# Sparse attention in a fused transformer layer: keys and values formed per head instead of queries and outputs in the latent space, and one more top-k inside the attention loop

## The chip, the cores and the metric

The kernel runs on one core of a Trainium2 chip. The metric is the device time of one execution in microseconds (us), lower is better. Before the change three executions took 1062.2, 1065.04 and 1066.31 us; the median is 1065.04 us.

## The reference, cut to what matters

One decoder layer on 512 tokens of width 1024: modulated RMSNorm, sparse attention beside a pooling mixer, both gated, an output projection, and then a mixture of 32 experts. The change touches only the attention (`SEQ` 512, `N_HEADS` 8, `HEAD_DIM` 64, `KV_LATENT` 128, `Q_BLOCK` 128, so `k_sel` is 128):

```python
score = einsum('bqhs,bqh->bqs', relu(raw), wi_b * IDX_W_SCALE)
score = where(causal[None], score, -inf)
_, idx = lax.top_k(score, k_sel)
kv_sel = vmap(lambda kv, i: kv[i])(ckv, idx)
q_lat = einsum('bqhd,lhd->bqhl', q_b, w_uk)
logits = einsum('bqhl,bqkl->bqhk', q_lat, kv_sel) * ATTN_SCALE
p = softmax(where(valid, logits, -inf))
o_lat = einsum('bqhk,bqkl->bqhl', p, kv_sel)
return einsum('bqhl,lhd->bqhd', o_lat, w_uv)
```

For a head, `q_lat . kv` is the same number as `q . (w_uk kv)`, and `(p kv) w_uv` the same as `p (kv w_uv)`. The order of the products can be chosen.

## The kernel before, in words

All of it is one program with an in-order instruction stream for each engine, written out by hand. There is no planner. Results of TensorE (PE) go through eight banks of PSUM. The list `JOBS` (lines 257 to 299) gives every PE result a number in the order in which PE makes them, and names the engine that empties it: "A" for ScalarE (ACT), "D" for VectorE (DVE). Job n lies in bank n % 8, and `start` (line 1549) makes PE wait until job n - 8 has been emptied. So the order of this list decides which old result a new one waits for.

Tokens come in four chunks of 128. A query of chunk ch sees keys 0 to 128 (ch + 1) - 1. The stages that matter, in the order of PE:

- `tok` (line 1611): the latent (`ckv`), the indexer's queries and keys and its weights, for each chunk; `uk` turns w_uk round; `tr` turns ckv and the indexer's operands (line 1621).
- `index_chunk(ch)` (line 1625): indexer products of chunk ch in four row groups. ACT takes their relu (line 867) into two alternating buffers, and DVE sums them with weights in `select(ch)` (lines 1163 and 1166). `take_best` (line 1178) is then one round per 8 of the 128 best: a MAX8 and a MATCH_REPLACE8 over the scores. Then one TENSOR_SCALAR makes the additive mask `bias_of[ch]`. Chunk 0 needs no choice. Chunk 1 is chosen in `select(1)`, chunk 2 in `select(2)`, both before the attention loop. Chunk 3 is only scored there (`apart=True`), and its 16 rounds are spread over iterations 0 to 4 of the loop (`TAKES`, line 1199).
- `q`, `pool`, `gb` and `ga` are projections "in parts" (`by_feature_parts`, line 1633): each weight block of 128 columns is split into a high and a low part. ACT writes the high part (`block_high`, line 841). The low part is a subtraction that GpSimd (POOL) does for `q`, `pool` and `gb` (`block_low`, line 648), and DVE for `ga` (line 1233). A block is 24 matmuls of 128x512.
- `qlat` (line 1653): per head, the query through w_uk: 8 fp32 matmuls that use 64 rows of PE each, two side by side.
- `ada` (line 1592), 12 pieces of the modulation vector, their row sums `row` (`ada_sum`, line 1667), added on DVE in `ada_rows` (line 1195).
- The attention loop (PE line 1685, ACT line 909, DVE line 1237) has 8 iterations g: chunk g // 2, four of the eight heads. In iteration g PE does: `PT` (line 1691, turn the four heads' probabilities, each waits for DVE), `L` of g + 1 (`logits`, line 1677, four fp32 matmuls over all 128 rows, 128 (ch + 1) keys wide), `O` (line 1697, one fp32 matmul of 128x512 per key block, the four heads side by side), `gb` of g + 1, in g 0 the four `z`, in odd g a `V` (line 1711, output through w_uv), in g 1 `ada_sum` 4 to 7, and in g 0 to 3 one `ada`. DVE does in iteration g: scale the four heads' exponentials (`RECIPROCAL` and `TENSOR_SCALAR`, lines 1242 and 1243), in g 2 `ada_rows`, then `maxima(g + 1)` (line 1209: mask, row maximum; this empties the logits), then its rounds of `TAKES`. ACT does: copy the `PT` results, copy `O`, exponentials of g + 1 (line 899), tanh of `gb` and the next `block_high` (lines 903 and 841).
- After the loop: 8 blocks `B` (96 matmuls), `ada_sum` 8 to 11, then the blocks `ga` and `A`, the output projection, the router and the experts. In the last iteration (g 7) ACT and DVE also split `zT` and the first weights of `B` (lines 919, 874, 1219, 1226); `B` waits for that.

POOL builds the pooled inputs dT (lines 664 to 670) between its `block_low` steps. It loads the bias rows (line 677) once the four `z` are done, and then does `block_low` of gb 2 and gb 3 back to back.

Of the kernel before, what the change touches and what calls it, by code (L numbers as in the profile page):

```python
# [27 lines left out]
P = 128  # L28
# [5 lines left out]
LAT = 128  # L34
# [32 lines left out]
def trunk(nc, x, c, norm1_g, norm2_g, w_ada, b_ada, w_in, kv_norm_g, w_uk, w_uv, w_pool, pool_scale,  # L67
# [3 lines left out]
    with ctx:  # L71
# [17 lines left out]
        T3 = sb("T3", [P, 3, T])  # L89
        ckv = sb("ckv", [P, C, LAT])  # L90
        wi = sb("wi", [P, C, IH])
        uvp = sb("uvp", [P, H, P])
# [63 lines left out]
        q_latT = hT  # L156
# [3 lines left out]
        dT = qT  # L160
# [7 lines left out]
        o_latT = attn[:, 2048:3072].rearrange("p (h q) -> p h q", h=H)  # L168
# [13 lines left out]
        uk = small[:, 0:512]  # L182
        ukT = area_b[:, 512:1024].rearrange("p (i t) -> p i t", i=4)
# [66 lines left out]
        def piece(kind, i=0):  # L250
# [9 lines left out]
                + [("tok", i, "D") for i in range(C)] + [("uk", 0, "A")] + [("tr", i, "A") for i in range(C)]  # L260
                + [("idx", 4 + i, "A") for i in range(4)]
                + [("q", 0, "A"), ("q", 1, "A"), ("ada", 4, "A"), ("q", 2, "A"), ("q", 3, "A"), ("ada", 5, "A")]
                + [("qlat", h, "A") for h in range(H)]
# [4 lines left out]
        JOBS += [("L", i, "D") for i in range(4)] + [("gb", 0, "A")]  # L268
        for g in range(NGR):
# [8 lines left out]
            if g % 2:  # L278
                JOBS += [("V", g // 2, "A")]
            if g == 1:  # L280
                JOBS += [("row", j, "D") for j in range(4, 8)]
            if g < 4:
                JOBS += [("ada", 8 + g, "A")]
        JOBS += [("B", m, "D") for m in range(KD)]
        JOBS += [("row", j, "D") for j in range(8, 12)]
# [17 lines left out]
        def bank(kind, i=0):  # L303
            return ps[:, number[kind, i] % 8, :]
# [277 lines left out]
        def _(pool):  # L582
# [16 lines left out]
            link(nc.gpsimd.memset(uvp[:, :, :], 0.0))  # L599
# [35 lines left out]
            for h in range(H):  # L635
                at = HD * (h % 2)
                pool.dma_start(uvp[:, h, at:at + HD], w_uv[0, :, h, :]).then_inc(uv_in, 16)
# [17 lines left out]
            for g, w in enumerate(WINDOWS):  # L655
                block_low(block_no["pool", g] + 2)
                pool.wait_ge(by_act, emptied[number["pool", g]])
                if g == 0:
                    pool.wait_ge(job_done, number["qlat", H - 1] + 1)
# [22 lines left out]
            pool.wait_ge(job_done, number["V", C - 1] + 1)  # L682
# [110 lines left out]
        def _(act):  # L793
# [58 lines left out]
            nc.scalar.activation(ukT[:, :, :].rearrange("p a l -> p (a l)"), job("uk"), ACT.Copy).then_inc(by_act, 1)  # L852
# [24 lines left out]
            index_chunk(1)  # L877
            for i in range(4):
# [4 lines left out]
            for h in range(H):  # L883
                nc.scalar.activation(q_latT[:, h, :], job("qlat", h), ACT.Copy).then_inc(by_act, 1)
# [21 lines left out]

            exponentials(0)
            gate_b(0)
            for g in range(NGR):
# [13 lines left out]
                if g == 0:  # L923
                    act.wait_ge(d_ok, PG)
                nc.scalar.activation(o_latT[:, 4 * hh:4 * hh + 4, :].rearrange("p h q -> p (h q)"),
                                     job("O", g), ACT.Copy).then_inc(by_act, 1)
# [7 lines left out]
                if hh:  # L934
                    nc.scalar.activation(oT[:, :, ch * P:(ch + 1) * P],
                                         job("V", ch).rearrange("p (a q) -> p a q", a=4),
                                         ACT.Copy).then_inc(by_act, 1)
# [158 lines left out]
        def _(dve):  # L1096
# [56 lines left out]
            def select(ch, apart=False):  # L1153
# [3 lines left out]
                s = score[:, 0:n]  # L1157
                for h in range(IH):
# [5 lines left out]
                    else:  # L1164
                        to = r if apart and h == IH - 1 else s
# [21 lines left out]
            select(2)  # L1187
# [10 lines left out]
            last_scores = relu[:, 1, :]  # L1198
            TAKES = (3, 4, 3, 3, 3)
# [37 lines left out]
            for g in range(NGR):  # L1237
# [7 lines left out]
                if g == 2:  # L1245
                    dve.wait_ge(brow_in, 32)
                    for j in range(4, 8):
                        ada_rows(j)
                if g < NGR - 1:
                    maxima(g + 1)  # L1250
# [4 lines left out]
                if g < len(TAKES):  # L1255
                    take_best(last_scores, TAKES[g])
                if g == len(TAKES) - 1:
                    link(v.tensor_scalar(bias_of[C - 1], last_scores, 2 * MASKED, HIDDEN, ALU.is_gt, ALU.mult))
# [10 lines left out]
            for j in range(8, 12):  # L1269
# [709 lines left out]
```

## Time and profile before

| | us |
|---|---|
| median of three executions | 1065.04 |
| profiled execution, its own time | 1059.28 |
| its span in the profile | 1057.4 |
| TensorE busy (share) | 988.0 (93%) |
| VectorE busy (share) | 781.2 (74%) |
| ScalarE busy (share) | 558.6 (53%) |
| GpSimd busy (share) | 212.3 (20%) |

Times in the views count from the start of the span. The indexer and `q` begin near 61 us, the attention loop near 130 us. The loop's last `gb` block ends at 229.49 us, `B` runs to 260.48 us, and the part with the experts takes the rest from about 400 us on. A matmul's shown duration contains its latency, so the shown durations of neighbours overlap; the distance of starts, or the merged pieces of the chain of waits, gives the rate. One fp32 matmul counts as two instructions there.

### The profile page before, as it was taken

To read this page: it belongs to the slowest core of one execution; us is meant where nothing else is said; L and a number is where in the kernel's file an instruction comes from. 1 tells how busy PE (TensorE), PEld (TensorE's weight loads), DVE (VectorE), ACT (ScalarE), POOL (GpSimd) and SP (SyncE) were. 2 spreads that over 40 slices of the span, in tenths; PEclk is the share of its full clock that TensorE was granted. 3 is DMA by queue.
4 is the path that set the end of the run, shared out by engine and by line. 5 is a ranking of instruction groups with operands and counts; after the bars stand their busy time and mean duration, and the time that the engine had idled before them with its cause. 6 is when DMAs were issued, how large, how long until landed. Compare 5 with 4: busy or idle time off the path is not lost.

```text
span 1057.4 us, 13833 instructions
## 1 busy us (share of the span) xinstructions
PE 988.0 (93%) x4467; PEld 665.7 (63%) x4467; DVE 781.2 (74%) x1116; ACT 558.6 (53%) x840; POOL 212.3 (20%) x237
## 2 busy tenths in 40 slices
PE   3889899999999983899999999999999999999995
PEld 2666566667887553566666666666666665666652
DVE  0474967535435657789898898889989889898885
ACT  6334443543223232466675666756666675766742
POOL 1233931105100012111211212121121211212100
PEclk9899999999999995899999999999999999999998
DMA  9826625502306457479999999999999999999745
GB/s 345 294 81 239 239 81 205 188 6 95 133 27 239 162 220 247 160 281 365 380 341 382 363 369 363 353 376 359 364 358 357 374 356 362 363 361 366 240 129 195
DMA packets 63208, 283.29 MB, mean 268 GB/s; under 512 B 7488, under 2 KB 8796, under 8 KB 38600
## 3 DMA queue, kind: packets, MB, share of 16 engines
q1 hardware_dynamic: 53528, 257.93, 65.2%
q0 software_dynamic: 9648, 24.94, 9.0%
q8 instruction: 19, 0.31, 0.1%
q14 instruction: 13, 0.11, 0.0%
HBM read 272.62 MB, written 18.56 MB: 275 GB/s over the span
## 4 chain that ended last, share of the span: by engine, by line
PE 85%; DVE 5%; DMA 4%; issue 2%; ACT 2%; POOL 0%; SPq 0%; DVEq 0%; ACTq 0%; POOLq 0%
PE ps L1828 32%; PE ps L1563 19%; PE ps L1890 10%; PE ps L1884 8%; DMA X<-in_w_down_dram 3%; PE ps L1762 2%; PE ps L1773 2%; PE ps L1592 2%; PE ps L1799 2%; PE ps L1611 2%; PE ps L1677 2%; PE ps L1806 1%; PE ps L1864 1%; DVE whl L1302 1%; DMA X<-in_x_dram 1%
## 5 line engine op out<-in xcount | busy, mean ns | idle before, releaser
L1828 PE MATMUL ps<-whl,xhl 128*96 128x512 f32 x1536 | 369.6, 399 | 0.0
L1302 DVE TENSOR_TENSOR whl<-ring,whl 128x1024 fp32r<-128x1024 f32 x256 | 304.2, 1221 | 53.5 <-ACT whl L961 52.6
L1828 PEld LDWEIGHTS ps<-whl,xhl 128*96 128x96 f32 x1536 | 250.3, 163 | 108.3 <-issue 0.4
L961 ACT ACTIVATE whl<-ring 128x1024 fp32r<-128x1024 f32 x256 | 267.4, 1060 | 56.2 <-PE ps L1828 47.4
L1563 PE MATMUL ps<-h_hi,wb_hl 128*128 128x512 f32 x384 | 127.1, 404 | 1.2 <-POOL wb_hl L648 1.2
L1890 PE MATMUL ps<-X,attn 128*96 128x512 f32 x256 | 115.4, 594 | 0.7 <-DMA X<-in_w_down_dram 0.7
L729 POOL DMA_INDIRECT moe_rows<-mix,ius x31 | 46.3, 1494 | 298.6 <-DVE mix L1445 150.2
L1884 PE MATMUL ps<-whl,ahl 128*96 128x512 f32 x384 | 97.2, 402 | 2.9 <-DVE whl L1302 2.9
L1563 PEld LDWEIGHTS ps<-h_hi,wb_hl 128*128 128x128 f32 x384 | 72.9, 190 | 22.2 <-issue 5.1
L1302 DVE TENSOR_TENSOR whl<-X,whl 128x1024 fp32r<-128x1024 f32 x64 | 78.3, 1225 | 8.8 <-ACT whl L961 7.9
L961 ACT ACTIVATE whl<-X 128x1024 fp32r<-128x1024 f32 x64 | 67.9, 1062 | 20.0 <-PE ps L1828 20.0
L1890 PEld LDWEIGHTS ps<-X,attn 128*96 128x96 f32 x256 | 41.6, 164 | 57.3 <-issue 51.1
L1884 PEld LDWEIGHTS ps<-whl,ahl 128*96 128x96 f32 x384 | 60.4, 164 | 26.0 <-issue 3.1
L1563 PE MATMUL ps<-h_lo,wb_hl 128*128 128x512 f32 x192 | 75.7, 394 | 0.0
L1035 ACT ACTIVATE attn<-ps 128x192 f32<-128x192 f32 x32 | 10.6, 330 | 91.4 <-PE ps L1864 91.4
L648 POOL TENSOR_TENSOR wb_hl<-ring,wb_hl 128x1024 fp32r<-128x1024 f32 x16 | 38.5, 2414 | 90.1 <-ACT wb_hl L841 72.1
L1445 DVE SCALAR_TENSOR_TENSOR mix<-ps,WC,attn 96x512 f32<-96x512 f32 x64 | 44.8, 740 | 10.7 <-PE ps L1890 10.7
L759 POOL COPY ius<-idx 128x1 uint32 (+1 forms) x31 | 14.3, 460 | 161.4 <-DMA moe_rows<-mix,ius 161.4
L1563 PE MATMUL ps<-zo_hl,wb_hl 128*128 128x512 f32 x192 | 44.9, 390 | 0.0
L723 POOL DMA_INDIRECT apad<-h_rows,iug x32 | 39.7, 1241 | 25.0 <-POOL iug L750 24.4
L841 ACT ACTIVATE wb_hl<-ring 128x1024 fp32r<-128x1024 f32 x24 | 25.2, 1055 | 36.6 <-PE ps L1563 32.7
L1563 PEld LDWEIGHTS ps<-h_lo,wb_hl 128*128 128x128 f32 x192 | 36.5, 190 | 9.0 <-issue 1.9
(248 smaller groups left out, 1169.7 us busy)
## 6 DMA issues: line engine op xcount, KB each, us to landing
ring<-in_w_gu_dram SPq DMA_DIRECT2D x128, 1024.0 KB, 9.8
X<-in_w_down_dram SPq DMA_DIRECT2D x64, 1024.0 KB, 10.2
ring<-in_w_ada_dram SPq DMA_DIRECT2D x12, 2048.0 KB, 12.0
ring<-in_w_in_dram SPq DMA_DIRECT2D x6, 2048.0 KB, 8.0
ring<-in_w_out_dram SPq DMA_DIRECT2D x2, 2048.0 KB, 8.1
X<-in_x_dram SPq DMA_DIRECT2D x1, 2048.0 KB, 8.0
ring<-in_w_b_up_dram SPq DMA_DIRECT2D x1, 2048.0 KB, 14.2
ring<-in_w_a_up_dram SPq DMA_DIRECT2D x1, 2048.0 KB, 8.0
```

Of the source, the lines that this page charges most:

```text
L648: nc.gpsimd.tensor_tensor(wb_hl[:, buffer_of(BLOCKS[n]), 1, :, :], block_w(n), wb_hl[:, buffer_of(BLOCKS[n]), 0, :, :], ALU.subtract).then ...
L723: pool.indirect_dma_start(out=XG[0:slots, b, :], out_offset=None, in_=h2_dram, in_offset=bass.IndirectOffsetOnAxis(ap=iug[0:slots, b:b + 1 ...
L729: pool.indirect_dma_start(out=y_dram, in_=Y[0:slots, b, :], in_offset=None, out_offset=bass.IndirectOffsetOnAxis(ap=which, axis=0), bounds ...
L841: nc.scalar.activation(wb_hl[:, buffer_of(BLOCKS[n]), 0, :, :], block_w(n), ACT.Copy).then_inc(b_hi_ok, 1)
L961: nc.scalar.activation(whl[:, buf, 0, :], part, ACT.Copy).then_inc(hi_ok, 1)
L1302: v.tensor_tensor(whl[:, buf, 1, :], part, whl[:, buf, 0, :], ALU.subtract).then_inc(lo_ok, 1)
L1445: last = v.scalar_tensor_tensor(out=Y[0:slots, b, sl], in0=ps[0:slots, 2 + half, :], scalar=WC[0:slots, b:b + 1], in1=g2b[0:slots, sl], op ...
L1563: last = mm(out_, a, b, start=(n == 0 and start_), stop=(n == len(pairs) - 1))
L1592: last = mm(b_[at:at + 32, :], cnd[:, 2, k:k + 1].broadcast_to([P, 32]), w[:, k, :], start=(k < 4), stop=(k >= 4), tile_position=(0, at))
L1828: last = mm(ps[0:slots, half, :], xhl[:, a, k, :], whl[:, at, b, half * CH:(half + 1) * CH], start=False, stop=(k == KD - 1 and a == 1))
L1884: last = mm(ps[0:slots, 2 + half, :], ahl[:, a, i, :], whl[:, at, b, half * CH:(half + 1) * CH], start=(i == 0 and a + b == 0), stop=False)
L1890: last = mm(ps[0:slots, 2 + half, :], actT[:, k, :], down_part(k)[:, half * CH:(half + 1) * CH], start=False, stop=(k == KF - 1))
```

## The change

Keys per head (`kT`: four matmuls, w_uk by ckvT) are formed once after `index_chunk(1)`, and values per head (`V`: four matmuls, ckvT by w_uv) once after the first logits. `uk`, `qlat` and the four `V` of the loop go. `L` takes 64 rows of PE per head, even and odd heads in the two row halves. `O` is done per head with 64 columns of weights and 128 of queries, even and odd heads in the two column halves, and gives the attention output itself. Chunk 2 is now only scored before the loop; its 16 rounds are done in iterations 0 and 1, and those of chunk 3 in iterations 2 to 4. `ada_sum` 8 to 11 move from behind `B` into iteration 5, their additions on DVE into iteration 6. The banks of all jobs are shifted by the same number so that the last job keeps its bank.

```diff
-        T3 = sb("T3", [P, 3, T])
-        ckv = sb("ckv", [P, C, LAT])
+        V = sb("V", [P, C, AW])
-        uvp = sb("uvp", [P, H, P])
+        uvp = sb("uvp", [P, 2, AW])
...
-        q_latT = hT
+        T3 = V[:, 0:3, :]
+        ckv = V[:, 3, :].rearrange("p (c l) -> p c l", c=C)
+        kT = hT[:, 0:PG, :]
-        dT = qT
+        dT = hT[:, PG:2 * PG, :]
...
-                + [("tok", i, "D") for i in range(C)] + [("uk", 0, "A")] + [("tr", i, "A") for i in range(C)]
-                + [("idx", 4 + i, "A") for i in range(4)]
+                + [("tok", i, "D") for i in range(C)] + [("tr", i, "A") for i in range(C)]
+                + [("idx", 4 + i, "A") for i in range(4)] + [("kT", a, "A") for a in range(PG)]
-                + [("qlat", h, "A") for h in range(H)]
-        JOBS += [("L", i, "D") for i in range(4)] + [("gb", 0, "A")]
+        JOBS += [("L", i, "D") for i in range(4)] + [("V", s_, "A") for s_ in range(C)] + [("gb", 0, "A")]
-            if g % 2:
-                JOBS += [("V", g // 2, "A")]
+            if g == 5:
+                JOBS += [("row", j, "D") for j in range(8, 12)]
-        JOBS += [("row", j, "D") for j in range(8, 12)]
-            return ps[:, number[kind, i] % 8, :]
+            return ps[:, (number[kind, i] - len(JOBS)) % 8, :]
...
             index_chunk(1)
+            act.wait_ge(h_lo_ok, 1)
+            for a in range(PG):
+                nc.scalar.activation(kT[:, a, :], job("kT", a), ACT.Copy).then_inc(by_act, 1)
-            for h in range(H):
-                nc.scalar.activation(q_latT[:, h, :], job("qlat", h), ACT.Copy).then_inc(by_act, 1)
+            act.wait_ge(job_done, number["V", C - 1] + 1)
+            for s_ in range(C):
+                nc.scalar.activation(V[:, s_, :], job("V", s_), ACT.Copy).then_inc(by_act, 1)
             exponentials(0)
             gate_b(0)
-                nc.scalar.activation(o_latT[:, 4 * hh:4 * hh + 4, :].rearrange("p h q -> p (h q)"),
-                                     job("O", g), ACT.Copy).then_inc(by_act, 1)
+                nc.scalar.activation(oT[:, 2 * hh:2 * hh + 2, ch * P:(ch + 1) * P],
+                                     job("O", g)[:, 0:2 * P].rearrange("p (a q) -> p a q", a=2),
+                                     ACT.Copy).then_inc(by_act, 1)
...
-            select(2)
+            select(2, apart=True)
             select(3, apart=True)
-            TAKES = (3, 4, 3, 3, 3)
+            scores_of = {2: bias_of[2], 3: relu[:, 1, :]}
+            TAKES = ((2, 8, False), (2, 8, True), (3, 5, False), (3, 6, False), (3, 5, True))
+                if g == 6:
+                    for j in range(8, 12):
+                        ada_rows(j)
                 if g < len(TAKES):
-                    take_best(last_scores, TAKES[g])
-                if g == len(TAKES) - 1:
-                    link(v.tensor_scalar(bias_of[C - 1], last_scores, 2 * MASKED, HIDDEN, ALU.is_gt, ALU.mult))
+                    sc, times, whole = TAKES[g]
+                    take_best(scores_of[sc], times)
+                    if whole:
+                        link(v.tensor_scalar(bias_of[sc], scores_of[sc], 2 * MASKED, HIDDEN, ALU.is_gt, ALU.mult))
...
+            pe.wait_ge(uk_in, 16)
+            for a in range(PG):
+                mm(start("kT", a), uk[:, a * P:(a + 1) * P], ckvT, start=True, stop=True).then_inc(job_done, 1)
-                    mm(b_[:, 0:P * (ch + 1)], q_latT[:, h, ch * P:(ch + 1) * P], ckvT[:, 0:P * (ch + 1)], start=True,
-                       stop=True).then_inc(job_done, 1)
+                    r = slice(HD * (h % 2), HD * (h % 2) + HD)
+                    mm(b_[:, 0:P * (ch + 1)], qT[r, h // 2, ch * P:(ch + 1) * P], kT[r, h // 2, 0:P * (ch + 1)], start=True,
+                       stop=True, tile_position=(HD * (h % 2), 0)).then_inc(job_done, 1)
             logits(0)
+            pe.wait_ge(uv_in, 16)
+            for s_ in range(C):
+                mm(start("V", s_), ckvT[:, s_ * P:(s_ + 1) * P], uv, start=True, stop=True).then_inc(job_done, 1)
             gate_b(0)
-                chain(b_, [(ckv[:, s, :], pT[:, s, :, :].rearrange("p h q -> p (h q)")) for s in range(ch + 1)], job_done)
+                for a in range(2):
+                    for s in range(ch + 1):
+                        for q in range(2):
+                            h, at = 4 * hh + 2 * a + q, HD * q
+                            last = mm(b_[at:at + HD, a * P:(a + 1) * P], V[:, s, h * HD:(h + 1) * HD], pT[:, s, 2 * a + q, :],
+                                      start=(s == 0), stop=(s == ch), tile_position=(0, at))
+                if g == 5:
+                    for j in range(8, 12):
+                        ada_sum(j)
-            for j in range(8, 12):
-                ada_sum(j)
```

## Rows read from the trace of the kernel before

**Rows 1.** The page, the chain that ended last, shares of the span.

```profile
PE 85%; DVE 5%; DMA 4%; issue 2%; ACT 2%; POOL 0%; SPq 0%; DVEq 0%; ACTq 0%; POOLq 0%
```

**Rows 2.** Chain of waits in order of time: start us, length us, what.

```profile
62.58 12.77 PE ps L1563 x48
...
90.20 3.63 PE ps L1653 x16
...
128.21 0.29 DVE attn L1209
...
144.80 1.85 PE ps L1592 x16
146.66 0.59 PE ps L1691 x4
...
200.81 1.31 PE ps L1691 x12
...
217.16 3.44 PE ps L1677 x8
...
229.49 0.02 issue
...
236.66 23.82 PE ps L1563 x112
260.48 3.44 PE ps L1667 x8
```

**Rows 3.** Groups by shape up to 330 us: busy us, mean ns, idle before.

```profile
L1563 PE MATMUL ps<-attn,ckv 128*128 128x512 f32 x40 | 18.8, 600 | 1.0 <-ACT attn L914 1.0
L1563 PE MATMUL ps<-attn,uvp 128*128 128x128 f32 x64 | 7.9, 276 | 0.8 <-ACT attn L925 0.8
```

**Rows 4.** Timeline of PE: start us, length us, in brackets idle before.

```profile
62.58 0.47 PE L1563 MATMUL ps<-h_hi,wb_hl 128*128 128x512 f32 x1 [1.20 <-POOL wb_hl L648]
```

**Rows 5.** Windows of the trace: length, busy time by engine, PE's granted clock.

```profile
64.00:65.00 1.00, 1.00 (x3) 0.73 (x3) 1.00 (x1) 0.00 (x0) 0.82 (x1) 0.50 0.19 74
...
134.00:134.50 0.50, 0.50 (x4) 0.50 (x4) 0.43 (x5) 0.00 (x0) 0.00 (x0) 0.50 0.00 0
```

**Rows 6.** Timeline of DVE: top-k rounds of widths 384 and 512.

```profile
98.56 0.56 DVE L1180 MAX8 top<-small 128x8 f32<-128x384 f32 x1
...
99.81 0.56 DVE L1180 MAX8 top<-small 128x8 f32<-128x384 f32 x1
...
178.90 0.69 DVE L1180 MAX8 top<-small 128x8 f32<-128x512 f32 x1
...
180.40 0.69 DVE L1180 MAX8 top<-small 128x8 f32<-128x512 f32 x1
```

**Rows 7.** Timeline of DVE: the other steps of an iteration.

```profile
159.94 2.58 DVE L1195 TENSOR_TENSOR small<-ps,small 1x512 f32<-1x512 f32 x4
...
176.06 0.56 DVE L1209 CUSTOM_DVE_ANT_0 attn<-ps,maskb 128x384 f32<-128x384 f32 x1 [3.28 <-PE ps L1677]
...
176.78 0.56 DVE L1209 CUSTOM_DVE_ANT_0 attn<-ps,maskb 128x384 f32<-128x384 f32 x1
...
183.44 0.16 DVE L1242 RECIPROCAL am<-am 128x1 f32<-128x1 f32 x1
...
183.97 0.15 DVE L1242 RECIPROCAL am<-am 128x1 f32<-128x1 f32 x1
```

**Rows 8.** Timeline of all engines: DVE and POOL at 156 us, ACT before.

```profile
155.86 1.05 ACT L841 ACTIVATE wb_hl<-ring 128x1024 fp32r<-128x1024 f32 x1
...
156.85 0.35 DVE L1243 TENSOR_SCALAR attn<-attn,am 128x256 f32<-128x256 f32 x1
...
156.99 2.42 POOL L648 TENSOR_TENSOR wb_hl<-ring,wb_hl 128x1024 fp32r<-128x1024 f32 x1 [5.67 <-ACT wb_hl L841]
...
157.31 2.25 DVE L1243 TENSOR_SCALAR attn<-attn,am 128x256 f32<-128x256 f32 x1
```

**Rows 9.** Timeline of POOL behind the four z.

```profile
146.61 4.71 POOL L648 TENSOR_TENSOR wb_hl<-ring,wb_hl 128x1024 fp32r<-128x1024 f32 x2
```

## What the change will do: the prediction

> **What bounds the kernel now.** I read the page's chain first: PE holds 85% of the span [rows 1]. Then the chain in order of time, from the indexer to the end of `B` [rows 2]. PE follows PE almost throughout. The one stretch where another engine decides is 118 to 133 us, when DVE scores chunk 3 and starts the first maxima at 128.21. From 146.66 (start of the turns of iteration 1) to 229.49 (end of the last `gb`) PE is never released by DVE. So work taken from PE shortens the kernel until DVE becomes late, and the question is how much room DVE has when 16 more rounds come into the loop. The groups by shape [rows 3], the windows with the clock [rows 5] and the timelines of DVE and POOL [rows 6 to 9] give the prices.
>
> **PE, what goes and what comes.** `qlat` goes, 3.63 us [rows 2]. `uk` is four turns at 0.11 (1.31 / 12), 0.44 [rows 2]. `L`: 3.44 for four heads of 512 keys [rows 2], by width 0.86 (ch + 1), and two of each, 17 us. `O`: 20 matmuls of 0.86 (an `ada_sum` of four such takes 3.44 [rows 2]), 17 us. `V`: 32 small ones, 64 instructions at 0.107 (this is the rate of the first 16 of the 112 in [rows 2]), 6.8 us [rows 3]. `kT` and `V` are new, 3.44 each. If row halves and column halves run side by side, `L` and `O` cost half, 8.6 each. `qlat` shows it for row halves: eight matmuls of 512 in 3.63, half of 8 x 0.86. `ada` shows it for column groups: eight of 512 columns in 1.85, a quarter of 6.9 [rows 2]. PE sheds 45 and gains 24: 21 us less work. The trace has no fp32 matmul of 64 weight columns with 128 moving ones. Its price lies between half of 0.214 (perfectly paired) and the whole 0.214 that the unpaired 128x128 costs. I take half and keep the other end below as a rival.
>
> Each `L` and `O` now changes the shape in which PE is divided. `ada` with its two such changes takes 1.85 where a quarter of 8 x 0.853 is 1.71, so about 0.07 a change [rows 2]. The Trainium skill (TensorEngine Tiling (Array Packing), section Key Properties) says that changing the tiling mode drains TensorE, which speaks against this change. By the row, the nine changes where PE is the bound below would add 0.6 us. By a drain as long as a whole 128-column matmul (0.21) it would be 2 us. No row separates the drain from the matmul, and the sum leaves it out.
>
> **Before the loop.** PE idles 1.20 us before `q` [rows 4]; `kT` fills it. So the first maxima move by -3.63 - 0.44 - 1.20 + 3.41 = -1.9. The clock adds to this. At 64 us PE is granted 0.50, the 1.2 GHz level [rows 5], after idling between the turns. Two blocks with an `ada` there (a block is 24 matmuls at 0.227, from 96 of them in some 22 us behind 238 [rows 2]) take 12.77 for the blocks where 10.9 is full speed, so it costs 1.7. With `kT` in the gap it may stay at 2.4 GHz (-3.5 in all) or not (-1.9); I take -2.7. The eight ACT copies of `qlat` become four of `kT` and hide under `q`. Scoring chunk 2 alone frees DVE at about 98, which gains nothing, since chunk 3 waits for PE. DMA: one issue for w_uv in place of eight on POOL at 40 us, hidden.
>
> **The first iteration, the bank.** `gb` 0 ran while DVE scored. It is now number 8 behind `L` 0, so its bank is that of `L` 0, and it waits for the first maxima to empty it. `V` fills 3.4 of the shadow, then PE idles some 2.9 us and `gb` 0 (5.45) is exposed. It ends at 128.21 - 2.7 + 0.3 + 5.45 = 131.3. Such an idle stretch preceded the 0.50 at 134 us [rows 5]; a slow stretch costs up to 1.7, I take 1.2: G = 132.5. Queued behind it on PE are the four turns and `L` of iteration 1, for which DVE waits; on ACT, tanh, `block_high` and the copies of the turns.
>
> **The loop, DVE.** A round is 1.25 at width 384 and 1.51 at 512 [rows 6]. Scaling four heads is 4 x 0.53 = 2.1 at 384, maxima 4 x 0.72 = 2.85 [rows 7]. A narrower chunk saves about 0.13 a head and step, by the two MAX8 widths [rows 6]. `ada_rows` is 2.6 [rows 7]. Between the last scaled head and the next maxima lie a turn and the first `L`, 0.8 to 1.2. Let S(g) be the start of scaling in iteration g.
> - S(1) = G + 1.05 + 1.8 + 8 x 1.25 = G + 12.85. PE needs 13.8 to `ada` 8's end, about level.
> - S(2) = S(1) + 1.6 + 0.8 + 2.3 + 10.0 + 0.4 (mask) = + 15.1.
> - S(3) = + 1.9 + 2.6 + 2.3 + 5 x 1.51 = + 14.4.
> - S(4) = + 1.9 + 1.1 + 2.85 + 6 x 1.51 = + 14.95.
> - S(5) = + 2.1 + 1.2 + 2.85 + 7.6 + 0.45 = + 14.2.
>
> PE needs only 12.5, 9.9, 10.3 and 9.3 in these four (turns, halved `L` and `O`, `gb` 5.45, `ada_sum` 3.44, `ada` 1.85). So PE waits 16 us and DVE is the bound: 58.65 where PE took 54.15 before (146.66 to 200.81 [rows 2]). S(5) = 132.5 + 12.85 + 58.65 = 204.0.
>
> **Two prices on top.** First, a TENSOR_SCALAR of DVE that meets POOL's `block_low` waits for its end: 2.25 in place of 0.35, over at 159.56, POOL at 159.41 [rows 8]. The MAX8 at 512 keep their 0.69, so only masks and scaling are exposed. POOL starts 1.75 after a `gb` block ends (tanh and the 1.05 of ACT [rows 8]). With PE done early and DVE's scaling last, the two meet: worked out, scaling 3 meets `gb` 5's step (about 1.7), mask and scaling 5 meet `gb` 7's (1.6), scaling 4 just misses (0.4). In iteration 1 POOL's double step begins 1.8 after the last `z` (144.80, 146.61 [rows 2, 9]), at G + 13.7, in the middle of scaling 1 (G + 13.0 to 14.4). That costs 0 to 4.7, I take 2.9. Together 6.6, with bounds 0 and 11. Second, the clock: PE idles 1.5 to 4 us in each of iterations 2 to 5, and turns and `L` on DVE's path then run at 1.2 GHz, 0.3 to 0.9 each: 1.6, bounds 0 and 4. S(5) = 212.2.
>
> **The rest.** From S(5) PE is the bound again: scaling and turns 2.6, `L` 1.7, `O` 1.3, `gb` 5.45, `ada_sum` 3.44, turns 1.75, `L` 1.7, `O` 1.7, `gb` 5.45 = 25.1, and 1.5 for one slow stretch (bounds 0 and 1.7). The last `gb` ends at 238.8, before 229.49 [rows 2]: +9.3. Behind it `B` waited until 238.4 (236.66 and the 16 small matmuls). Without `V` its start is set by ACT splitting zT, DVE's part of it and the first weights, some 1 us sooner. But PE idles 3.4 us there, and a slow stretch takes 1.3 back: +0.3. `ada_sum` behind `B` is gone, -3.44 [rows 2]; the first `ga` weights must be ready without its cover, and by the rates (ACT 1.05, DVE 1.2 after block 6 of `B`) they just are; missing it costs under 1. From there all is as before. Sum: +9.3 + 0.3 - 3.4 = **+6.2**. The profiled execution took 1059.28 (span 1057.4), so it would become 1065.5. The median of the runs is 1065.04, 5.8 above it, and I put the same difference on it: **1071**.
>
> **Rivals.**
> - *Ports and clock miss.* DVE bounds the loop as above, but `block_low` falls between the scalings and PE stays at 2.4 GHz. Without the extras: first maxima -3.5, G = 130.5, last `gb` 227.1 (-2.4), tail -1.05, `ada_sum` -3.44: -6.9 at best, 1058; with some of them, up to 1065; 1061 stands for it. For it: before, only one scaling in the loop was hit for long. Against: PE had no idle time there then.
> - *PE's saving comes through.* If DVE hid its rounds, PE's 16 us of waiting would be saved on top of -6.9, about 1043. Against: DVE's sums are of durations that hardly vary.
> - *The low clock feeds itself (slower).* In iterations 1 to 4 PE has 2.6 to 5 us to spare. A slow stretch costs 1.7, as the first one did, two cost 3.4; where an iteration has as much as 7 us at 1.2 GHz the slack is used up and `gb` ends late, POOL's step with it. Price: 1.5 an iteration more, +6 on the forecast, 1077. For it: both low windows of [rows 5] followed idle stretches as short as those here. Against: PE is mostly busy after each.
> - *The halves don't overlap* as written. DVE's path hardly feels it (one head of `L` is no slower), but iterations 5 and 6 pay 3.4 for `L` and 3.0 for `O`: 1077.5. Against: `qlat` and `ada`.
>
> **Numbers.** Forecast 0.47 (own range 1066 to 1076), ports and clock miss 0.25, saving through 0.05, low clock 0.17, halves 0.06. A measurement tells about 0.5% (5.3 us) from no change. Of the forecast 0.27 lies above 1070.3, with the last two that makes slower 0.50. Of the first rival 0.10 lies below 1059.7, with the second faster 0.15. The same: 0.35. The range leaves out the second rival and the outer tails: 1058 to 1080.
>
> **What would show it.** In the changed profile: DVE nearly unbroken from the first maxima 1 to scaling 5; PE idle before the turns of iterations 2 to 5, released by DVE line 1243; `gb` 0 released by the maxima; granted clock of 0.5 in several windows between 125 and 245; TENSOR_SCALARs of 1 to 2.4 us beside `block_low`; last `gb` at 235 to 242. It is wrong if PE's busy tenths stay at 9 through the loop, or if the last `gb` ends before 230.

## The result and the profile after

The changed kernel takes 1072.32 us (median of four runs, 1072.27 to 1072.45) where the kernel before, run beside it, takes 1065.22: a ratio of 1.0099, 95% interval 1.0073 to 1.0124. A later job gave 1071.58 against 1061.0, ratio 1.0095 [1.0069, 1.012]. It is slower by about 1%. The forecast was 1071, in a range of 1058 to 1080.

The profiled execution took 1072.3, its span is 1070.0. That is 12.6 more than the span of before, while the medians lie 7.1 and 10.6 apart: the profiled execution of before (1059.28) was one of its quicker ones.

The shares of the chain that ended last, to be held against [rows 1], and the page's busy times and granted clock of the changed kernel:

```profile
PE 981.7 (92%) x4519; PEld 657.7 (61%) x4519; DVE 787.2 (74%) x1116; ACT 556.0 (52%) x835; POOL 205.3 (19%) x229
PEclk9899989989999997789999999999999999999998
PE 81%; DVE 10%; DMA 3%; issue 3%; ACT 2%; POOL 0%; SPq 0%; DVEq 0%; ACTq 0%; POOLq 0%
```

PE lost 4 points of the chain, and DVE has 10% of it. Next comes that chain in order of time (start, length, what), to be held against [rows 2]:

```profile
128.13 5.75 PE ps L1558 x24
147.23 5.33 DVE attn L1236
152.69 1.24 PE ps L1683 x3
153.93 1.20 PE ps L1666 x4
182.45 1.57 DVE attn L1236
186.19 2.45 PE ps L1666 x8
215.32 1.72 DVE maskb L1255
217.82 2.79 PE ps L1683 x12
220.62 2.68 PE ps L1666 x8
223.30 1.46 PE ps L1694 x24
224.76 5.68 PE ps L1558 x24
230.44 3.44 PE ps L1654 x8
239.44 5.70 PE ps L1558 x24
253.05 6.98 PE ps L1558 x23
```

L1558 is a block or its part, L1683 the turns, L1666 `L`, L1694 `O`, L1654 `ada_sum`, L1236 DVE's scaling, L1255 the mask; the last line is the first blocks of `B`. The first line is `gb` 0, released by the first maxima as forecast. Between 147 and 217 us the chain runs through DVE (scaling, maxima, rounds), and PE has only the turns and `L` between the scaling and the next maxima in it. The last `gb` ends at 239.44 + 5.70 = 245.1; before it ended at 229.49.

What PE waited for between 118 and 250 us (us in total, number of waits, longest):

```profile
PE ps L1683 <- DVE attn L1236: 16.1, 5, 5.1
PE ps L1558 <- DVE am L1202: 2.5, 1, 2.5
PE ps L1694 <- ACT attn L910: 1.2, 1, 1.2
```

The forecast had PE waiting 16 us for DVE in iterations 2 to 5. It waited 16.1, but in all five iterations from 1 to 5, and 4.6 of it in iteration 1. That the two numbers agree is in part luck.

The windows of before, then of after (from:to, length; busy us of PE, PEld, DVE, ACT, POOL with counts; granted clock; DMA share; GB/s):

```profile
118.00:250.00 132.00, 127.00 (x599) 86.59 (x598) 82.52 (x234) 61.54 (x148) 38.94 (x30) 0.99 0.35 124
```

```profile
118.00:250.00 132.00, 110.21 (x618) 71.10 (x617) 100.19 (x272) 58.04 (x142) 29.77 (x22) 0.92 0.34 120
216.00:218.00 2.00, 0.17 (x1) 0.21 (x2) 1.89 (x5) 0.00 (x0) 0.74 (x1) 0.50 0.12 13
218.00:220.00 2.00, 2.00 (x11) 1.98 (x11) 1.19 (x5) 0.98 (x2) 0.00 (x0) 0.50 0.89 285
220.00:222.00 2.00, 2.00 (x7) 1.06 (x8) 0.00 (x0) 0.98 (x2) 0.00 (x0) 0.50 1.05 410
```

In this stretch DVE is busy 17.7 us more, PE 16.8 us less, and the granted clock falls from 0.99 to 0.92. The 16.8 us are mostly waits, not saved work: of the whole execution PE is busy 981.7 us, before 988.0. The three small windows show how this is paid. PE is idle (0.17 of 2 us) behind DVE's mask and scaling 5, the clock is at 0.50, the 1.2 GHz level, and there it stays while PE does the turns and `L` that DVE waits for.

The long TENSOR_SCALAR that the forecast spoke of, on DVE and with it the step of GpSimd that it met (start, length, engine, line, operation):

```profile
146.84 0.28 DVE L1236 TENSOR_SCALAR attn<-attn,am 128x128 f32<-128x128 f32 x1
147.23 5.32 DVE L1236 TENSOR_SCALAR attn<-attn,am 128x128 f32<-128x128 f32 x1
```

```profile
147.81 4.64 POOL L643 TENSOR_TENSOR wb_hl<-ring,wb_hl 128x1024 fp32r<-128x1024 f32 x2
```

Two heads of one shape: 0.28 and 5.32. The second ends at 152.55, GpSimd's two steps at 152.45. It starts at 147.23, 0.58 us before the first of the two steps in GpSimd's records; what holds it in that time the trace doesn't show.

### The profile page after: what moved, and what is told of

Its sections match the earlier page's. It is cut to its first block, busy times and chain, and to the rows that moved or that the text cites. A ratio compares the mean times of both kernels' runs of the same rounds, so it can differ in the third digit from the quotient of the medians.

```text
span 1070.0 us, 13914 instructions
## 1 busy us (share of the span) xinstructions
PE 981.7 (92%) x4519; PEld 657.7 (61%) x4519; DVE 787.2 (74%) x1116; ACT 556.0 (52%) x835; POOL 205.3 (19%) x229
## 4 chain that ended last, share of the span: by engine, by line
PE 81%; DVE 10%; DMA 3%; issue 3%; ACT 2%; POOL 0%; SPq 0%; DVEq 0%; ACTq 0%; POOLq 0%
PE ps L1820 32%; PE ps L1558 14%; PE ps L1882 10%; PE ps L1876 8%; PE ps L1754 2%; PE ps L1765 2%; PE ps L1791 2%; DVE top L1173 2%; PE ps L1606 2%; PE ps L1798 1%; PE ps L1587 1%; DMA X<-in_w_down_dram 1%; DVE small L1174 1%; PE ps L1666 1%; PE ps L1856 1%
## 5 line engine op out<-in xcount | busy, mean ns | idle before, releaser
L1558 PE MATMUL ps<-h_hi,wb_hl 128*128 128x512 f32 x384 | 123.9, 396 | 2.5 <-DVE am L1202 2.5
L1558 PEld LDWEIGHTS ps<-h_hi,wb_hl 128*128 128x128 f32 x384 | 72.2, 188 | 23.5 <-issue 5.0
L1558 PE MATMUL ps<-h_lo,wb_hl 128*128 128x512 f32 x192 | 74.9, 390 | 0.0
L1028 ACT ACTIVATE attn<-ps 128x192 f32<-128x192 f32 x32 | 10.6, 332 | 90.8 <-PE ps L1856 90.8
L1558 PE MATMUL ps<-zo_hl,wb_hl 128*128 128x512 f32 x192 | 46.4, 399 | 3.3 <-DVE wb_hl L1219 3.3
L1558 PEld LDWEIGHTS ps<-zo_hl,wb_hl 128*128 128x128 f32 x192 | 37.1, 194 | 11.3 <-issue 3.5
```

The lines of the kernel that those rows point to most:

```text
L1558: last = mm(out_, a, b, start=(n == 0 and start_), stop=(n == len(pairs) - 1))
```

## Experiments

"Ctl" is the changed kernel once more; the others are edits of it unless their text says otherwise. All ran beside the kernel before (1061.0 us in the first job, 1061.38 in the second, 1062.31 in the third, 1062.61 in the fourth). S(g) is the start of scaling in iteration g, as in the prediction. Ctl ran in the first job alone. Where a run of a later job is compared with it, its distance from its own before is given too; ctl is +10.6 us from its before.

**ctl**, unedited.

> The changed kernel itself, unedited, so that the others of this job have it beside them. Both theories: 1072 us, within 1 us of its first runs, 5 to 9 us over the kernel before.

Measured: 1071.58 (eight runs, 1068.6 to 1076.2). In its profile `gb` 0 takes 7.18 us where it took 5.75 in the first profile. The low clock falls on other pieces from run to run, so single steps are compared with that in mind.

**dve_before**: the rounds of chunk 2 go back ahead of the loop, and the heads' new form stays.

```diff
-            select(2, apart=True)
+            select(2)
...
-            TAKES = ((2, 8, False), (2, 8, True), (3, 5, False), (3, 6, False), (3, 5, True))
+            TAKES = ((3, 3, False), (3, 4, False), (3, 3, False), (3, 3, False), (3, 3, True))
```

> The changed kernel with the 16 rounds of chunk 2 back before the loop and the rounds of chunk 3 as before (3, 4, 3, 3, 3). Theory A (VectorE bounds iterations 1 to 4 of the changed kernel): VectorE's share of these iterations falls by 20 us of rounds, PE becomes the bound or nearly so (iterations of 13.8, 12.5, 11.4, 10.4 and 11.1 us), PE's idle stretches shrink, the clock stays high and the scaling no longer meets GpSimd's steps: 1052 to 1058 us, 15 to 20 under the changed kernel and under the kernel before too. Theory B (the rounds are hidden in the loop, and the loss comes from gb 0 waiting for a bank and from the new shapes of the matmuls): the rounds were free where they are, so 1069 to 1073, no gain. Before the loop both expect at most 2 us of delay, since the rounds end near 119 us and chunk 3's relu near 120.

Measured: 1052.54, ratio 0.9897 [0.9861, 0.9933]. Without the rounds in the loop the change makes the kernel 8.5 us faster than before; the rounds in the loop cost 19 us on top. The loss is DVE's in the loop. The 8.5 us are those of keys and values per head together with the moved `ada_sum` 8 to 11, which is still in this kernel; no run separates the two.

**before_top2**: the other half alone. The kernel before, with only the rounds of chunk 2 put into the loop by the lists of the changed kernel (and, as there, `select(2, apart=True)`, with the scores of chunk 2 kept in `bias_of[2]`).

```diff
-            TAKES = (3, 4, 3, 3, 3)
+            TAKES = ((2, 8, False), (2, 8, True), (3, 5, False), (3, 6, False), (3, 5, True))
```

> The kernel before with one part of the change alone: chunk 2 only scored before the loop, its 16 rounds in iterations 0 and 1, those of chunk 3 in iterations 2 to 4. PE's work stays as before. Theory A (VectorE becomes the bound wherever its chain is longer than PE's iteration): iterations 1 to 4 cost PE 15.7, 11.8, 14.5 and 12.1 us, VectorE's chain 15.1, 14.4, 14.9 and 14.2, so it adds about 5 us, and some 2 to 6 more for scaling that meets GpSimd and for the low clock: 1066 to 1072 where the kernel before takes 1061. Theory B (the rounds are hidden): within 1 us of the kernel before.

Measured: 1079.01, ratio 1.0156 [1.0117, 1.0196]. That is +17.6 against its own before, well above what was expected. The two parts together, -8.5 and +17.6, make +9.1, close to the +10.6 of ctl in the first job. The expectation (1066 to 1072) missed the size: it had 2 to 6 us in all for meetings with GpSimd and the low clock. The chain of this kernel has both (its profiled execution, 1083.09, is 4 us above its median): line 1243 is its scaling (the four longest pieces), line 1678 its `L` over all rows. The second line below is four heads of 256 keys: 3.43, where 4 x 0.43 = 1.7 is full clock ([rows 2], 0.86 for 512):

```profile
146.62 5.37 DVE attn L1243
152.57 3.43 PE ps L1678 x8
182.02 2.43 DVE attn L1243
200.37 1.21 DVE attn L1243
216.21 2.44 DVE attn L1243
```

**pool_apart**: GpSimd's low parts of `gb` 2 and `gb` 3 move ahead of its wait for `z` and the bias rows, so they are no longer back to back in front of scaling 1.

```diff
+            block_low(block_no["gb", 2])
+            block_low(block_no["gb", 3])
...
-            for n in range(block_no["gb", 2], block_no["ga", 0]):
+            for n in range(block_no["gb", 4], block_no["ga", 0]):
```

> The changed kernel with one thing moved: GpSimd does its steps for gb 2 and gb 3 before it waits for the last z and loads the bias rows, so they no longer meet VectorE's scaling in iteration 1 (a TENSOR_SCALAR of 5.3 us in the changed kernel). Theory A: 4 to 6 us faster, 1066 to 1068, and that TENSOR_SCALAR takes 0.3. Theory B (PE's own order sets iteration 1): within 1 us of the changed kernel.

Measured: 1064.87 (ten runs), 1.0035 [1.0014, 1.0056], 6.7 us less than ctl. Scaling 1 takes 0.29 a head (three of its four TENSOR_SCALARs in DVE's timeline, then GpSimd's step, which is over at 145.32, before the first head at 145.53):

```profile
145.92 0.29 DVE L1238 TENSOR_SCALAR attn<-attn,am 128x128 f32<-128x128 f32 x1
146.31 0.29 DVE L1238 TENSOR_SCALAR attn<-attn,am 128x128 f32<-128x128 f32 x1
146.71 0.28 DVE L1238 TENSOR_SCALAR attn<-attn,am 128x128 f32<-128x128 f32 x1
```

```profile
142.95 2.37 POOL L643 TENSOR_TENSOR wb_hl<-ring,wb_hl 128x1024 fp32r<-128x1024 f32 x1 [6.27 <-ACT wb_hl L836]
```

S(1) to S(2) takes 15.57 instead of the changed kernel's 21.27; the other steps stay within 0.7 us but for S(4) to S(5), 15.80 instead of 17.21. Of the 5.7 us, 5.0 are the meeting itself, and 0.7 the wait for the first `L` behind it, which the changed kernel does at the 1.2 GHz level and this one does not. DVE's wait there, in the changed kernel and in this one:

```profile
155.22 0.42 DVE L1202 CUSTOM_DVE_ANT_0 attn<-ps,maskb 128x256 f32<-128x256 f32 x1 [1.89 <-PE ps L1666]
```

```profile
148.21 0.42 DVE L1204 CUSTOM_DVE_ANT_0 attn<-ps,maskb 128x256 f32<-128x256 f32 x1 [1.22 <-PE ps L1668]
```

**gb0_first**: `gb` 0 ahead of `V` in the order of PE, so it waits for an older bank than that of `L` 0. ScalarE's exponentials and its work on `gb` 0 move ahead of its copies of `V` with it.

```diff
-        JOBS += [("L", i, "D") for i in range(4)] + [("V", s_, "A") for s_ in range(C)] + [("gb", 0, "A")]
+        JOBS += [("L", i, "D") for i in range(4)] + [("gb", 0, "A")] + [("V", s_, "A") for s_ in range(C)]
...
```

> The changed kernel with gb 0 ahead of the four V matmuls in the list of jobs, so that gb 0 runs in the shadow of the scoring and only the last V (0.9 us) waits for the first maxima. Iteration 0 then starts 3.5 us earlier. Theory A: VectorE's chain starts with it, so the whole gain arrives, or more or less than it as the scaling now meets GpSimd's steps at another place: 1067 to 1071. Theory B: about the same 3.5 us, 1068 to 1069. What tells them apart is the other kernels; this one measures the bank term, forecast at 5.5 us of exposed gb.

Measured: 1069.77 (nine runs), 1.0072 [1.0052, 1.0092], 1.8 less than ctl where 3.5 was expected; the intervals overlap. The first iteration is 1.6 us shorter (S(0) to S(1) 15.48 instead of 17.05), and scaling 1 still meets GpSimd (5.38). The exposed `gb` 0 is real but small in this kernel. In both, S(1) comes 11.76 us after the start of maxima 1 (134.88 to 146.64, here 131.88 to 143.64), the time of DVE's own maxima and rounds; what counts is only how much earlier maxima 1 can start, and behind the first maximum of all that was 1.8 us (5.32 instead of 7.11).

**warm**: PE does small matmuls without use (128x128, into a bank about to be overwritten) where it would idle ahead of the turns of iterations 1 to 5: 16, 5, 10, 14, 20 of them.

```diff
+            FILL = {1: 16, 2: 5, 3: 10, 4: 14, 5: 20}
...
+                    if i == 0:
+                        for _ in range(FILL.get(g, 0)):
+                            mm(b_[:, 0:P], ident[:, :], ones[:, :], start=True, stop=True)
```

> The changed kernel with filler matmuls of 128x128 (0.21 us each, into the bank that the turns then overwrite) on PE ahead of the turns of iterations 1 to 5: 16, 5, 10, 14 and 20 of them, where PE only waits for VectorE. It adds work and takes nothing away. If the low clock (1.2 GHz after PE idled) costs what the trace suggests, 1.2 to 2.4 us between the last scaled head and the next maxima in each of iterations 1, 3, 4 and 5 where full speed needs 0.8 to 1.2, plus slow starts of L and O: 4 to 7 us faster than the unedited changed kernel, 1065 to 1068. If the clock is only a sign and VectorE's instructions set the time by themselves: no gain, or a loss of up to 3 us where a filler runs too long.

Measured: 1072.22 (ten runs), 1.0095 [1.0067, 1.0123], +10.8 from its own before: nothing gained. By the steps, S(4) to S(5) shortened from 17.21 to 15.83 and S(5) to S(6) from 8.89 to 7.42, but S(3) to S(4) grew from 17.60 to 18.26: there the fillers stood in front of turns that were ready. The test was confounded, so it was made again.

**warm2**: fillers in iterations 1, 4 and 5 alone, in numbers that end before DVE's last scaled head.

```diff
+            FILL = {1: 16, 4: 12, 5: 18}
```

> The filler experiment again, mended: fillers only where PE idled longest (16 ahead of the turns of iteration 1, 12 in 4, 18 in 5), none in iterations 2 and 3. The first one gained 0.7, 1.3 and 1.5 us behind its fillers of iterations 1, 4 and 5, and lost 3 in iteration 3, where PE came late and the fillers stood in front of the turns. If the low clock costs what these stretches say (theory C): 2 to 4 us faster than the changed kernel's 1071.6 to 1072.3, and from the last scaled head to the next maxima in iterations 4 and 5 1.3 to 2 us in place of 2.9 and 3.3. If not: within 1 us of it.

Measured: 1067.41 (six runs), 1.0056 [1.0032, 1.008], +4.8 from its own before. That is 4.2 us less than ctl (5.8 by the distances from before), just over the expected 2 to 4. The two ran in different jobs and their intervals overlap (ctl 1.0069 to 1.012), so the size is uncertain, and the steps of the profile have to carry it. PE's timeline ahead of iteration 5, its window, and DVE's wait for the first `L`:

```profile
209.48 4.18 PE L1685 MATMUL ps<-ones,ident 128*128 128x128 f32 x36
214.65 2.19 PE L1688 MATMUL ps<-ident,attn 128*128 128x128 f32 x12 [0.99 <-DVE attn L1236]
```

```profile
216.00:218.00 2.00, 1.99 (x12) 1.07 (x12) 0.17 (x1) 1.29 (x3) 0.00 (x0) 1.00 1.00 381
```

```profile
218.04 0.69 DVE L1202 CUSTOM_DVE_ANT_0 attn<-ps,maskb 128x512 f32<-128x512 f32 x1 [1.86 <-PE ps L1666]
```

```profile
222.58 0.69 DVE L1202 CUSTOM_DVE_ANT_0 attn<-ps,maskb 128x512 f32<-128x512 f32 x1 [3.33 <-PE ps L1666]
```

The last line is the same wait in the changed kernel without fillers: DVE stands 3.33 us between its last scaled head and the first maximum at the 1.2 GHz level, 1.86 at 2.4 GHz. The waits behind scaling 1, 3, 4 and 5 are 0.7, 0.4, 0.9 and 1.5 us shorter than in the changed kernel, 3.4 together, so the low clock was part of its time. But the fillers did one thing more: scaling 3 no longer meets GpSimd's step (1.2 us) and mask 5 is 0.2 us shorter, since the two engines have shifted against each other. So about 1.4 us of what the profile gained is not the clock.

**unpaired**: dve_before with `O` ordered one column half after the other, so that no two halves can run side by side.

```diff
-                for a in range(2):
-                    for s in range(ch + 1):
-                        for q in range(2):
+                for q in range(2):
+                    for a in range(2):
+                        for s in range(ch + 1):
```

> The kernel with the rounds before the loop, in which PE is nearly the bound (1052.5 us), with the matmuls of O ordered by column half first, so that neighbours use the same half and can't run side by side. If the halves overlap as the trace suggests (16 matmuls of 128 columns in 1.90 us, 0.12 each), O takes 0.86 (ch + 1) in place of 0.43 to 0.47 (ch + 1): 8 us more PE work, 5 to 8 of it on the path, 1057 to 1060. If they don't overlap anyway: no difference, 1052 to 1053.

Measured: 1048.71, 0.9883 [0.9843, 0.9922]. This expectation fell: the kernel was not slower. The last `O` of the loop in the chains of dve_before and of unpaired:

```profile
220.40 1.90 PE ps L1694 x32
```

```profile
214.31 3.26 PE ps L1694 x32
```

16 matmuls of 128 columns take 1.90 in pairs (0.119 each) and 3.26 without (0.204 each). So the halves do overlap, and the rival that said they don't is out. But the time did not follow. From S(4) to S(6) dve_before took 25.5 us and unpaired 20.9, for two reasons. In dve_before scalings 4 and 5 each meet GpSimd's step, about 1.9 us each over the usual 0.42, and in unpaired neither does:

```profile
185.07 2.34 DVE L1236 TENSOR_SCALAR attn<-attn,am 128x384 f32<-128x384 f32 x1
198.69 2.31 DVE L1236 TENSOR_SCALAR attn<-attn,am 128x384 f32<-128x384 f32 x1
```

And the wait behind scaling 5 is 1.87 instead of 3.17, at the higher clock (that behind scaling 4 is 0.9 longer). Over 118 to 250 us the clock is 0.99 in place of 0.96. That the longer `O` kept the clock up is argued; the missed meetings, a matter of when the engines get there, weigh more. The two medians are not to be told apart (intervals overlap). The windows of dve_before and of unpaired:

```profile
118.00:250.00 132.00, 119.36 (x675) 79.80 (x674) 91.55 (x241) 60.08 (x148) 44.57 (x34) 0.96 0.35 124
```

```profile
118.00:250.00 132.00, 124.83 (x679) 88.11 (x676) 89.11 (x240) 58.46 (x146) 43.31 (x34) 0.99 0.33 116
```

**after_unpaired**: the same order in the changed kernel.

> The changed kernel with only O's matmuls ordered by column half, so that neighbours can't overlap and O costs 4 to 7 us more of PE. Where the rounds are before the loop that order was no slower, and its granted clock was 0.99 against 0.96 through the loop. Theory C (PE's idle time pulls the clock down, and work put into the idle time costs nothing and keeps it up): in the iterations that VectorE bounds the extra work is free and turns and logits run faster, in iterations 5 and 6, where PE bounds, it costs up to 3: 1067 to 1072, clock of the loop above the changed kernel's 0.92. Theory D (O's time counts wherever it stands): 4 us or more slower than the changed kernel, 1075 or more.

Measured: 1074.79, 1.0111 [1.0072, 1.0149], 3.2 us more than ctl (1.9 by the distances from before), between the two theories; the intervals overlap. The loop's clock is 0.94 instead of 0.92 (0.91 in ctl). Up to S(3), where DVE is the bound, no step changes by more than 0.03 us, so the longer `O` is hidden. S(3) to S(5) takes 1.1 us more, of it 1.2 in longer meetings with GpSimd (scaling 3 2.04 instead of 1.56, mask 5 2.42 instead of 1.71), and S(6) to S(7), where PE is the bound, 1.4 more.

**all3**, dve_before with pool_apart and gb0_first, then **all4**, with the order of unpaired too, then **all5**: in all4 the low parts of `gb` 4 to 7 move from GpSimd to DVE, behind maxima 3 to 6, so that in the loop no scaling can meet GpSimd's step for them.

```diff
-            for n in range(block_no["gb", 4], block_no["ga", 0]):
-                block_low(n)
...
+                if 2 <= g <= 5:
+                    block_low(g + 2, "gb")
```

> The changed kernel with all three edits: the rounds of chunk 2 back before the loop, GpSimd's steps for gb 2 and gb 3 ahead of the last z, gb 0 ahead of V. With the rounds gone from the loop (1052.5) the other two have less to give: the scaling of iteration 1 no longer ends last, so the GpSimd edit gives 0 to 2, the bank up to 3.5. Theory A: 1048 to 1052. Theory B, by which the bank and PE's order carry the loss, wants the full 3.5 of the bank here: 1049 or less.

> All three edits (rounds before the loop, GpSimd ahead of z, gb 0 ahead of V) and O ordered by column half. The first three gave 1050.6, the last with the rounds alone 1048.7, and there PE waited 4 us for GpSimd's gb 2 in iteration 1, which the second edit removes. Theory C: the gains add, 1045 to 1048. Theory D: 1053 or more, since O's extra time counts.

> The kernel with the four edits above, and the low parts of gb 4 to 7 taken from GpSimd and given to VectorE behind the maxima of iterations 2 to 5 (1.23 us each), so that no scaling meets a GpSimd step any more; before, scalings 4 and 5 held a TENSOR_SCALAR of 2.3 us each. If that meeting still ends last, 1 to 4 us faster than the kernel with four edits; if VectorE's extra 1.23 us an iteration ends last, 0 to 3 slower. I expect 1 to 2 faster, 1043 to 1047.

Measured: 1050.58 (0.9893 [0.9854, 0.9933]), 1049.41 (0.9894 [0.9842, 0.9945]), 1045.74 (0.9836 [0.9801, 0.9871]). The first two are not to be told from dve_before and unpaired alone: in dve_before scaling 1 meets no step of GpSimd, so the first edit has little left to give, and all4 missed its expected 1045 to 1048 slightly. All5 has the lowest median of the study, 1.6% below the kernel before and 2.4% below the changed one, but it is not to be told from all4: their intervals overlap and their profiled executions took 1046.44 and 1046.38. In all4's profile only one scaling of iterations 1 to 7 still met GpSimd (2.19 in iteration 2; the two of 2.3 that the expectation names are those of all3), so there was little left to gain. The loops of all4 and of all5, to be held against the windows of before and after above:

```profile
118.00:250.00 132.00, 127.92 (x703) 89.54 (x700) 89.12 (x243) 60.98 (x150) 45.17 (x36) 1.00 0.36 123
```

```profile
118.00:250.00 132.00, 126.92 (x702) 89.58 (x695) 92.02 (x246) 60.95 (x150) 35.09 (x32) 1.00 0.36 124
```

In both PE is busy 127 to 128 of 132 us again, at full clock, with DVE at 89 and 92.

## Why the prediction was right

*PE's ledger.* Right in kind, some 3 us too good. The halves overlap, in `O` and in `L`. But each `O` costs about 0.2 us more than 0.107 a matmul, whatever its size: in dve_before 0.66 for four matmuls and 1.02 for eight, then 1.90 for sixteen (above), where 0.43, 0.86 and 1.71 would be perfect.

```profile
136.65 0.66 PE ps L1694 x8
165.34 1.02 PE ps L1694 x16
```

An `L` at full clock does the same (1.92 for 512 keys where 1.7 was taken). Sixteen groups at 0.2 are the 3 us: by these figures the change takes some 18 us from PE, not 21 (an estimate). Such a cost per group fits the rule of the Trainium skill (TensorEngine Tiling (Array Packing), Key Properties) that a change of mode drains TensorE; the prediction, with 0.07 a change read from `ada`, left it out. That the 0.2 us are the drain is not shown, since no run changes the mode without changing the matmuls. The 0.853 in that reading stands in no row; with the 0.86 of [rows 2] it still comes out at 0.07.

*Before the loop.* The first maxima come at 127.77 where 128.21 stood: -0.4. In this profile the indexer's part starts 1.4 us later: PE stood idle for 3.2 us ahead of an `ada` at 31 us (2.4 before) and then did it at the 1.2 GHz level, in 3.58 in place of 1.92, work that this change doesn't touch. Without that it is -1.8, the lower end of the two considered (-1.9 to -3.5): the slow stretch at 62 us stayed, 0.50 from 62 to 64. In ctl, the same kernel, the clock is 1.00 there, and the first maxima come at 124.89, -3.3, the other end:

```profile
124.89 0.29 DVE attn L1202
```

So both ends are real, and the -2.7 between them belongs to neither. (The slow stretch of before cost 12.77 - 10.9 = 1.9, where the working says 1.7.)

*The bank of `gb` 0.* Right: it waits 2.5 us for the maxima, then runs exposed and ends at 133.88 (forecast 132.5, from first maxima that were 2.3 earlier). The slow stretch taken for it was not in this profile; in ctl's it was.

*DVE as the bound.* Right. G to S(1) was 12.76 (forecast 12.85). S(1) to S(5) was 146.64 to 217.06, 70.4, against 58.65 plus extras of 8.2, 66.9. The meetings with GpSimd are there in the places named: scaling 1 +5.0 (5.32 less 0.28), scaling 3 +1.2, mask 5 +1.3 (1.71 less 0.4), 7.5 together where 6.6 was taken. That scaling 3 met `gb` 5's step and mask 5 `gb` 7's is as worked out; scaling 5 met none. In iteration 1 the size was off, 5.0 for 2.9 and beyond the bound of 4.7, because the TENSOR_SCALAR waited through both of GpSimd's steps.

*The low clock, and what was left.* What is left of the 70.4 is 70.4 - 58.65 - 7.5 = 4.3, where 1.6 was taken. From S(5) to the last `gb` it took 28.1, where 25.1 plus 1.5 was forecast: 3.0 for 1.5. Together 7.3 us against 3.1, and here is the term whose size was off. The waits between the last scaled head and the next maxima say how much of it is the clock. Behind scaling 1, 3, 4 and 5 they are 1.89, 2.53, 2.86 and 3.32 us, and at full clock 1.22 and 1.65 (pool_apart, 1 and 4), 1.56 (all5, 3) and 1.87 (warm2, 5): 4.3 us more at the 1.2 GHz level, 2.9 of it before S(5) and 1.5 behind. The filler experiment took 3.4 of these back. The other 3.0 us are not the clock: the working took 0.8 to 1.2 for waits that are 1.2 to 1.65 at full clock (1.4 in all), and from S(5) on warm2, with the wait at full clock, still takes 26.6 where 25.1 was worked out (`L` 1.92, `O` 1.90 and `gb` 5.70 each a little over their prices). A mean of 0.92 over 132 us at levels of 1 and 0.5 is some 21 us at the low level. Windows of 1 us put it at 150 to 157, 184 to 188, 201 to 205 and 215 to 223 us: some 5 us of it PE is idle, and the rest is turns and `L`, in iteration 1 also `O`; the `gb` blocks run at full clock but for the start of one.

*The last `gb`* ended at 245.1 for 238.8: start of the loop 1.4, DVE's steps 3.5, the end of the loop 1.5.

*The tail.* From the last `gb` to the start of the output projection 97.5 us, before 100.4: -2.9, forecast -3.1 (+0.3 and -3.44). `ada_sum` 8 to 11 in iteration 5 took their 3.44 there, 230.44 to 233.87 in the chain. That they would be better left behind `B` was not tried.

*From the sum to the number.* The profiled pair lies 13.0 apart (the spans 12.6), the forecast +6.2. To that I added 5.8 for the distance between the profiled execution of before and its median. The changed kernel's profiled execution (1072.3) lies at its median. So the number of 1071 is nearer to 1072.3 than the working deserves: the sum was 6.8 short in its profiled execution (5.4 without the slow `ada` at 31 us), and the offset made most of that good. That is luck, not working. Against the medians the change is +7.1 in one job and +10.6 in the other.

*The rivals.* "Ports and clock miss" (1061) is out, both were there. "The saving comes through" (1043) is what the kernel comes near to when the rounds are not in the loop: dve_before 1052.5, all5 1045.7. "The low clock feeds itself" (1077) was part of the truth; 1.5 an iteration more was too much. "The halves don't overlap" is out (0.119 a matmul against 0.204).

## What to carry to other kernels

Taking work from the engine that bounds a loop and giving work to the next one in the same edit must be costed as two edits: here the first was worth -8.5 us (with `ada_sum` moved) and the second cost +17.6. Before filling the second engine, add up its chain per iteration (its rounds, what it waits for on the first, where it meets a third), and don't go by its busy share, which was only 76% (100.19 of 132 us) in the changed kernel's loop. When TensorE becomes the one that waits, look at the granted clock in small windows: here the turns and `L` on the other engine's chain were then done at half speed.

## What was not expected of the hardware

- A 128x128 TENSOR_SCALAR of DVE that met GpSimd's TENSOR_TENSOR ended only when two of them, back to back, were over: 5.32 us for 0.28. GpSimd was at the loads of the bias rows when it began. Those loads alone don't hold it: in pool_apart the heads at 145.53, 145.92 and 146.31 run beside the same loads (145.26 to 146.48) in 0.29 each. The next single steps cost 1.2 to 1.3, and up to 2.1 in other runs. A top-k step was not held up: here, in the changed kernel, the MATCH_REPLACE8 that began inside GpSimd's step keeps its usual length, and the mask behind it waits. DVE's and GpSimd's timelines:

```profile
213.80 0.69 DVE L1173 MAX8 top<-small 128x8 f32<-128x512 f32 x1
214.61 0.68 DVE L1174 MATCH_REPLACE8 small<-top,small 128x512 f32<-128x512 f32 x1
215.32 1.71 DVE L1255 TENSOR_SCALAR maskb<-small 128x512 f32<-128x512 f32 x1
```

```profile
214.40 2.34 POOL L643 TENSOR_TENSOR wb_hl<-ring,wb_hl 128x1024 fp32r<-128x1024 f32 x1 [15.11 <-ACT wb_hl L834]
```

- With useless fp32 matmuls in TensorE's gaps the kernel took 1067.41 us instead of 1071.58, some 3.4 us of it by shorter waits at the higher clock; the intervals of the two overlap.
- fp32 matmuls with 64 weight columns and 128 moving ones: in a group of sixteen 0.119 us each in pairs, 0.204 without; in a group of four 0.165 each (0.66 us). The dearer order cost nothing in the steps where TensorE had idle time.
